# Edges between the matrices of the second block: residual tiles scaled on GpSimd, a chunk split in two halves, products without a use in the pauses

## The reference, cut to what matters

```
for layer in range(2):
    h = rmsnorm(x, norm_mix_pre[layer])
    y = mix_even(h, ...) if layer % 2 == 0 else mix_odd(h, ...)
    x = x + rmsnorm(y, norm_mix_post[layer])
    h = rmsnorm(x, norm_ffn_pre[layer])
    f = swiglu(h, ...)
    x = x + rmsnorm(f, norm_ffn_post[layer])
```

## Time and profile before

| | us |
|---|---|
| median of 3 runs (lowest, highest) | 1710.19 (1709.97, 1711.96) |
| the profiled execution, its own time | 1709.77 |
| its span in the trace | 1707.9 |
| PE busy | 1646.5 (96%) |
| DVE busy | 1147.5 (67%) |
| ACT busy | 806.0 (47%) |
| POOL busy | 248.4 (15%) |

### The profile page before, as it was taken

How to read it: one execution, slowest core, us unless ns; L and a number is a source line. 1 busy time by engine, 2 the same in 40 slices (tenths; PEclk the granted TensorE clock), 3 DMA queues, 4 the chain that set the end, 5 groups by cost and what they waited for, 6 DMA issues and landing times.

```text
span 1707.9 us, 31396 instructions
## 1 busy us (share of the span) xinstructions
PE 1646.5 (96%) x13022; PEld 1590.6 (93%) x13022; DVE 1147.5 (67%) x1529; ACT 806.0 (47%) x1049; POOL 248.4 (15%) x228
## 2 busy tenths in 40 slices
PE   6999999999999999999989999997999999989998
PEld 6999998899999999998989998887999998989987
DVE  5556587785566755676786656776766568786664
ACT  5333474653334533464664335554434355454333
POOL 1000520400032000511230044231100020020000
PEclk9999999999999999999999999998999999999999
DMA  5455444444544455445455543442445543145553
GB/s 214 172 182 184 166 159 151 149 148 172 202 171 155 168 178 198 160 157 153 149 190 187 203 183 135 147 148 99 145 176 199 195 154 117 51 152 193 175 194 123
DMA packets 39154, 280.01 MB, mean 164 GB/s; under 512 B 4880, under 2 KB 6032, under 8 KB 8848
## 3 DMA queue, kind: packets, MB, share of 16 engines
q1 hardware_dynamic: 36896, 270.34, 44.4%
q0 software_dynamic: 2160, 8.29, 1.5%
HBM read 275.10 MB, written 1.05 MB: 162 GB/s over the span
## 4 chain that ended last, share of the span: by engine, by line
PE 78%; DVE 9%; ACT 7%; issue 3%; DMA 2%; POOL 1%; SPq 0%; DVEq 0%; ACTq 0%; POOLq 0%
PE bank L732 24%; PE bank L734 23%; PE bank L733 23%; DVE w_lo L2285 4%; ACT w_hi L1604 4%; ACT h L1662 1%; PE bank L1116 1%; ACT h_hi L1661 1%; DMA raw<-in_up_w 1%; POOL h L658 1%; PE bank L1145 0%; DMA u<-upad 0%; DVE inv_s L2445 0%; POOL acc L663 0%; PE bank L1102 0%
## 5 line engine op out<-in xcount | busy, mean ns | idle before, releaser
L2285 DVE TENSOR_TENSOR w_lo<-raw,w_hi 128x2048 fp32r<-128x2048 f32 (+3 forms) x236 | 570.6, 2418 | 256.3 <-ACT w_hi L1604 256.1
L732 PE MATMUL bank<-h_hi,w_hi 128*128 128x272 f32 (+1 forms) x2280 | 655.5, 287 | 16.9 <-DVE h_lo L2431 13.5
L734 PE MATMUL bank<-h_hi,w_lo 128*128 128x272 f32 (+1 forms) x2280 | 652.6, 286 | 0.0
L733 PE MATMUL bank<-h_lo,w_hi 128*128 128x272 f32 (+1 forms) x2280 | 651.1, 286 | 0.0
L1604 ACT ACTIVATE w_hi<-raw 128x2048 fp32r<-128x2048 f32 (+4 forms) x243 | 475.6, 1958 | 360.9 <-PE bank L734 225.2
L732 PEld LDWEIGHTS bank<-h_hi,w_hi 128*128 128x128 f32 x2280 | 432.4, 190 | 23.0 <-issue 16.7
L734 PEld LDWEIGHTS bank<-h_hi,w_lo 128*128 128x128 f32 x2280 | 432.6, 190 | 0.0
L733 PEld LDWEIGHTS bank<-h_lo,w_hi 128*128 128x128 f32 x2280 | 431.6, 189 | 0.1
L732 PE MATMUL bank<-g_hi,w_hi 128*128 128x272 f32 (+1 forms) x1136 | 328.3, 289 | 11.1 <-DVE w_lo L2285 8.1
L734 PE MATMUL bank<-g_hi,w_lo 128*128 128x272 f32 (+1 forms) x1136 | 323.6, 285 | 0.0
L733 PE MATMUL bank<-g_lo,w_hi 128*128 128x272 f32 (+1 forms) x1136 | 323.4, 285 | 0.0
(11 more groups left out here) (397 smaller groups left out, 1936.1 us busy)
## 6 DMA issues: line engine op xcount, KB each, us to landing
raw<-in_up_w SPq DMA_DIRECT2D x111, 1024.0 KB, 4.8
raw<-in_down_w SPq DMA_DIRECT2D x40, 1408.0 KB, 5.9
raw<-in_in_w SPq DMA_DIRECT2D x20, 1024.0 KB, 4.8
raw<-in_up_w SPq DMA_DIRECT2D x16, 1152.0 KB, 5.1
raw<-in_out_w SPq DMA_DIRECT2D x16, 1024.0 KB, 4.8
raw<-in_even_w SPq DMA_DIRECT2D x12, 1024.0 KB, 4.7
raw<-in_last_down SPq DMA_DIRECT2D x11, 1024.0 KB, 4.8
raw<-in_odd_w SPq DMA_DIRECT2D x6, 1024.0 KB, 4.8
```

Of the source, the lines that this page charges most:

```text
L732: pe.matmul(out, w[0], x[0], start=first, stop=False)
L733: pe.matmul(out, w[0], x[1], start=False, stop=False)
L734: return pe.matmul(out, w[1], x[0], start=False, stop=last)
L2285: last = dve.tensor_tensor(lo[:, b:n], raw[:, slot, b:n], hi[:, b:n].bitcast(F32), ALU.subtract)
```

## The change

1. **Scaling.** In all three `new_residual`s GpSimd multiplies tiles 4 to 7 by `std` (`scale_residual`, four instructions), as soon as VectorE has written new tile 0; VectorE waits for each of them (`hm_ready`) in place of its multiplications of pairs 4 and 5, 6 and 7.
2. **Halves.** In pauses B and D the spare chunk is split in two halves. ScalarE makes the first half of `wx_hi` where it made the whole, and the second one behind `std`. VectorE makes the first half of `wx_lo` where it made the whole, and the second one behind `low` of tile 1. TensorE waits for the first half ahead of tile 0 and for the whole ahead of tile 4.
3. **Products without a use.** At the head of `first_pair`, so in all four pauses, TensorE makes 24 products of 256 columns into bank 0, which the first product of the pair then overwrites.

```diff
+IDLE_PRODUCTS = 24
+HALVED = LAYERS + 1 + 1
...
+            def scale_residual(n):
+                pool.wait_ge(v_ready, KD * (n + 1) + 1)
+                for k in range(KD // 2, KD):
+                    pool.tensor_tensor(h[:, k, META:T], h[:, k, META:T], std[:, 0:S], ALU.mult).then_inc(hm_ready, 1)
...
                 add_tiles(squared, sq, S)
+                scale_residual(2 * layer)
                 add_tiles(squared, sq, S, KD)
                 if not layer:
                     add_tiles(squared, sq, S)
+                    scale_residual(1)
...
+            def keep_multiplying():
+                pe.wait_ge(w_ready, chunk_is_split(0))
+                for _ in range(IDLE_PRODUCTS):
+                    pe.matmul(ps[0][:, 0:S], w_hi[:, st.wslot(0), 0:P], g_hi[:, 0, 0:S], start=True, stop=True)
...
-            def first_pair():
-                pe.wait_ge(w_ready, chunk_is_split(1))
+            def first_pair(halved=False):
+                keep_multiplying()
+                if halved:
+                    pe.wait_ge(half_ready, HALVED + seen.next(half_ready))
+                else:
+                    pe.wait_ge(w_ready, chunk_is_split(1))
                 weights = (wpair(st.wslot(0), 0, UP_BLOCKS), (wx_hi, wx_lo))
                 for k in range(KD):
+                    if halved and k == KD // 2:
+                        pe.wait_ge(w_ready, chunk_is_split(1))
...
             def ffn_s(by_token=False):
-                first_pair()
+                first_pair(True)
...
-            def last_squares(after, bank):
+            def last_squares(after, bank, halved=False):
...
-                split_next(after, 0, 2, True)
+                if halved:
+                    split_next(after, 0, 2, True, 0).then_inc(half_hi, 1)
+                else:
+                    split_next(after, 0, 2, True)
...
-                        last_squares(UP_BLOCKS, ps[5])
+                        last_squares(UP_BLOCKS, ps[5], True)
...
                 else:
                     deviation(S)
+                    split_next(blocks, 0, 1, True, 1)
...
                 if scaled:
                     split_next(blocks, 0, 0)
-                split_next(blocks, 0, 1, True)
-                if scaled:
+                    split_next(blocks, 0, 1, True)
                     deviation_in()
                 else:
+                    slot, half = st.slot(1), blocks // 2 * P
+                    dve.wait_ge(half_hi, HALVED + seen.next(half_hi))
+                    dve.tensor_tensor(wx_lo[:, 0:half], raw[:, slot, 0:half], wx_hi[:, 0:half].bitcast(F32),
+                                      ALU.subtract).then_inc(half_ready, 1)
                     dve.wait_ge(var_ready, seen.next(var_ready))
...
                     if k < 2:
                         link(dve.tensor_tensor(xk(k), xk(k), std[:, 0:S], ALU.mult))
+                    elif k >= KD // 2:
+                        dve.wait_ge(hm_ready, seen.next(hm_ready))
                     elif k % 2 == 0:
...
                     if k:
                         low(k - 1, col + 8)
+                    if k == 2 and not scaled:
+                        split_next(blocks, 0, 1, True, 1)
```

## The result

| | before | after |
|---|---|---|
| median of 10 runs each, side by side (lowest, highest) | 1711.98 (1709.97, 1717.60) | 1715.64 (1713.19, 1718.08) |
| ratio of the two | | 1.0022 [1.0014, 1.0030] |
| the profiled execution, its own time | 1709.77 | 1717.94 |
| its span | 1707.9 | 1716.0 |
| PE busy | 1646.5 | 1659.0 |

The change makes the kernel slower by 0.2%: 3.7 us, with 2.4 to 5.1 inside the interval. I had forecast 1.1 us less. With ten runs the kernel before stands at 1712 and not at the 1710.2 of three, so 1.8 of the 6.5 us between 1709.1 and 1715.64 are the baseline's.

A forecast was written before the change was run, and what follows sets the result against it. TensorE's own work was taken to bound the kernel, with half-clock stretches at the pauses. A -0.7, B -0.4, C -0.1, D +0.1 gave -1.1 us, so a median of 1709.1 us, range 1705.4 to 1713.1.

The forecast's parts named there:

- Clock held in the pauses: All four pauses: 24 products without a use keep TensorE at the full clock, PEclk 1.00, costing nothing on time.
- The rival in which the products don't hold it: Pauses: pairs run as slowly as before but start later, C by 0.9, B by 0.2; +1.1, 1711.3 us; chance 0.12.
- Pause A, -0.7, "that is all that changes": Pause A: full clock alone ends the pair at about 1066.5 instead of 1067.20, -0.7 us, bound by VectorE's tile 1.
- A tile's 12 products, 1.38 us: TensorE in the pairs: each tile takes 1.38 us at full clock, so seven take 9.66 and six 8.28.
- Scaling, 1.76 given back of 1.90: Pauses: VectorE sheds 1.90 us of multiplications; four GpSimd instructions beside it cost 0.44 each, 1.76.
- Tile 0 at 3.2, tile 1 at 5.44 behind the first multiplication: Pauses with scaling: VectorE's low parts of tiles 0 and 1 come 3.2 and 5.44 us after the first multiplication.
- Pause C, -0.1: Pause C, scaling and held clock without halves: pair ends at 1400.86 against 1400.97, -0.1 us.
- the step that called the gain row's load free: Pause C: the load GpSimd issues behind the scaling is for the last matrix; no cost was counted.
- Halves: Pauses B and D: first multiplication 0.67 earlier in B, second half 1.32 us, pair 16.43 behind; B -0.4, D +0.1.
- The two engines hardly meet: Pauses B, C, D: VectorE and GpSimd meet at price 0; -5.8 with A's -0.7, 1704.4 us; chance 0.18.
- The starved start brings the clock down: TensorE's waits around tiles 0 to 2 lower the clock, 1.7 us per pause; all four 1715.9 us; chance 0.08.
- the far end of my own case: Pauses: 0.73 us per meeting makes C 1.1, B 1.0, D 1.5 later; +2.9 with A, 1713.1 us.

The follow-up runs named there:

- two later kernels: Against the kernel before: products in B to D with GpSimd's sums begun after new tile 7, 1714.33 us; products in all pauses plus 12 in the mixer, 1708.55 us.
- a third of nearly the same kernel: The changed kernel with GpSimd's issue of the gain row's load moved ahead of pause C; one run, 1712.26 us.
- the second time: The changed kernel run once more without an edit, beside the kernel before: 1714.10 us, ratio 1.0011.

## Why the prediction was wrong, step by step

- **Clock held in the pauses: right.** PEclk is 1.00 through all four pairs. The rival in which the products don't hold it falls, though they failed to in D of two later kernels.
- **Pause A, -0.7, "that is all that changes": this step failed by its sign.** A's pair gained 0.4 (the other 0.3 is the pace of the tiles, below). The sum stopped at the end of the pair; behind it the even mixer pays at least 1.5 us for a fall of the clock that the kernel before had in A and now has at the wait for `inv_s`. Net +1.1 and, in the two profiles of the changed kernel, more (the mixer is 3.0 and 4.4 longer; a third of nearly the same kernel has 1.5). The rest is more time at half: 10.2 us near 1152 in both profiles instead of 6.8, and in the first 6.8 us behind `inv_s` instead of 3.4. It comes and goes from profile to profile, and why is open.
- **A tile's 12 products, 1.38 us: mis-sized.** That was the pace of one tile. Seven tiles took 9.94 and not 9.66, six took 8.53 and not 8.28, so every pair ends some 0.25 to 0.3 later for the same hand-over.
- **Scaling, 1.76 given back of 1.90: mis-sized at both ends.** The 1.22 us pair in the earlier trace rows was itself beside GpSimd, and such a meeting does not leave with the instruction that it hit. Two pairs unhindered are 1.4 (0.68 and its gap, twice). And each of the four meetings is 0.48 (0.47 becomes 0.95), 1.9 in all, where I had 0.44 and 1.76. So VectorE's loop grows by 0.5, measured in B and D at 12.60 - 12.09 and 12.63 - 12.12, where I had a gain of 0.14.
- **Tile 0 at 3.2, tile 1 at 5.44 behind the first multiplication:** tile 0 came at 3.17 to 3.19. Tile 1 came at 5.97 with the issue of the gain row away, 6.43 with it: GpSimd, slowed to 0.94 an instruction, was still in its scaling when VectorE came to the pair, to new tile 2 and to the low part of tile 1.
- **Pause C, -0.1: measured +1.2.** Half of it is the step that called the gain row's load free because its data is for the last matrix. Its issue is an instruction in GpSimd's queue, and the scaling put it where VectorE is met (0.49). The rest is tile 1 (5.97 for 5.44) and the pace of the tiles.
- **Halves:** the first multiplication came earlier by 0.68 in B, as predicted (0.67); the second half took 1.21 (predicted 1.32); tile 2 was at 8.36 (8.1), and the pair at 16.9 (16.43). B came out at +0.1 for -0.4, and D at +0.7 for +0.1, both half by VectorE's longer way to tile 2 and half by the pace of the tiles behind it. (For D, 1.5 of the pause less 0.8 ahead of it, as the sum is earlier too.)
- **Sum:** A and mixer +1.1 or more, B +0.1, C +1.2, D +0.7: +3.1 us, where the runs show 3.7 and, the second time, 2.6 between the medians (ratios 1.0022 and 1.0011). It was -1.1.
- **The rivals.** "The two engines hardly meet" is wrong in every row. "The starved start brings the clock down": TensorE waited 1.13 and 0.72 in B, and the clock stayed at 1.00. The rule of the Trainium skill, TensorE: Matmul & The Clock Gate, section "A second HAM failure mode: psum-queue depth-cycling", by which short and frequent idling makes the clock swing, did not decide in the place where I had weighed it. I had priced the far end of my own case (0.73 for a meeting) at +2.9; the measured sum has that size, but from other terms.

The rows bear on a second page. The Trainium skill, SBUF — State Buffer, section "Who interferes with whom", says that a VectorE instruction with two inputs in SBUF contends with a GpSimd instruction that reads it. Of VectorE's two-port modes it adds that whoever issues first holds the shared ports for its whole instruction and the other blocks. For GpSimd as the loser the trace agrees: 2.60 us for a sum of 0.74, which ended 0.60 behind the split. For VectorE as the loser it shows 0.48 added, less than the 0.73 of a whole GpSimd instruction; whether VectorE had stood still for the rest of one, the rows don't show. My upper bound of 0.73 was not reached.

## What to carry to other kernels

Before work is moved from VectorE to GpSimd, count each moved instruction at what it costs VectorE as a meeting, here 0.48 us where shedding half of a 0.68 us pair saves 0.35, and look at which tiles are met first; a row that already stands beside the other engine is no price for what shedding it saves. When a pause is filled to hold the clock, follow the clock to the next wait: the fall may only move there, where here it cost more (1.5 us for the 0.4 gained). A DMA that GpSimd issues is work in its queue, wherever its data goes.

## What the runs showed of the hardware that I had not expected

- The same wait of 1.45 us was followed by a half-clock stretch with pause A filled, and by none where the clock had fallen in A, with one exception among thirteen profiles. Each 3.4 us more at half went with 1.1 to 1.7 us more of the even mixer.
- Which engine pays a meeting depends on the instructions: beside VectorE's rows of 256 elements both are slowed (0.48 to 0.95, 0.73 to 0.94); a GpSimd sum that began beside its split of 2048 elements took 2.60 us instead of 0.74 and ended 0.60 behind the split.
- GpSimd reading one row twice met VectorE at 0.24 to 0.42 us an instruction instead of 0.48 (3.25 us for its four instead of 3.74), in one kernel; the cause was not tried.
